# Layer 2's modulation summed partly by VectorE in the dense experts; first projection and S5's weights woven

## The chip, the cores and the metric

One core of one Trainium2 chip. The metric is the device time of one execution in microseconds, as a median of runs. The engines are TensorE (PE, matrix products), VectorE (DVE), ScalarE (ACT), GpSimd (POOL) and SyncE (SP, which here issues the weight loads). They run in parallel, each in its own program order, and wait for each other only through semaphores.

## The reference

Two blocks, each of two layers, on one sequence of 256 tokens with 1024 columns, all fp32. The change touches the first block, whose layer is:

```python
c_act = jax.nn.silu(c)
for layer in range(DEPTH):
    mod = c_act @ mod_w[layer] + mod_b[layer]
    sh_m, sc_m, gt_m, sh_f, sc_f, gt_f = jnp.split(mod[:, None, :], N_MOD, axis=-1)
    h = x * (1 + sc_m) + sh_m
    u, q, k, v, g_out, a_low = jnp.split(h @ w_in[layer], IN_SPLITS, axis=-1)
    y_s5 = _s5_group(u, ...)
    y_gla = _gla_group(q, k, v, g_out, a_low, ...)
    y = jnp.concatenate([y_s5, y_gla], axis=-1) @ w_out[layer]
    x = _layer_norm(DN_ALPHA * x + (1 + gt_m) * y, ...)
    h = x * (1 + sc_f) + sh_f
    ...
    f = _swiglu(h, ...) if layer % 2 == 0 else _moe_swiglu(h, ...)
    x = _layer_norm(DN_ALPHA * x + (1 + gt_f) * f, ...)
```

`c` is one row of 1024 values and `mod_w` is 2 x 1024 x 6144, so each layer's modulation is a product of one row with 24 MB of weights. S5 is a state space model with 32 groups (its weights are built from small parameters by elementwise work and transposes), GLA a gated linear attention with 4 heads. Layer 1 has a dense feed-forward part of width 3584 ("dense experts" below), layer 2 eight sparse experts of which two are chosen per token. The second block has two layers with three kinds of attention, a memory attention and a feed-forward part of width 4096.

## The kernel before, in words

**Products in fp32.** Each weight tile of 128 x 1024 values is split: ACT copies it to a high part (`his`, L303, tile WH), DVE subtracts that from the original to get a low part (`los`, L312, tile WL), and PE makes three products (`mm3`, L207: high by high, high by low, low by high). Weights come through a ring of five slots of 1 MB (tile RG), planned as one list of loads in the order of use (`plan`, L246); `fetch` (L291) lets SP issue a load once the load five places before it in the list has been released by DVE (or, for raw loads that PE reads as they are, by PE). Four pairs of conversion buffers lie between the ring and PE: ACT writes one when PE has released it.

**Modulation.** The 6144 columns of a layer are twelve blocks of 512. For each block PE multiplies the eight 128-row parts of two raw loads by one column of silu(c) (`pe_mod`, L517) into one PSUM bank; ACT copies the row out and sends it to DRAM (`a_mod`, L531). Shifts and scales come back as columns (`a_cols`, `pe_cols`, `v_cols`, L543 to L559), the two gates as rows spread over the partitions, to which DVE adds bias and 1 (`a_gate` L567, `v_gate` L575). Blocks 0 to 3 of layer 1 come in the start; blocks 4 to 11 of layer 1 and 0 to 3 of layer 2 in the first mixer stage; blocks 4 to 11 of layer 2 in the second.

**Stages.** A fence (L159) makes every engine wait for every other. Before the first mixer stage: a start (S5's parameter rows, `v_s5_rows`, L990; input weights, `v_s5_in`, L1129; four blocks of modulation), a fence, the first projection (`pe_project`, L620, with S5's fourteen transposing and multiplying jobs of layer 1 between its column blocks, `pe_s5_jobs`, L1082), and then S5's output weights on DVE (`v_s5_out`, L1159). S5's weights of layer 2 are built by DVE in the first mixer stage (input) and in the first three blocks of the dense experts (output).

**Mixer stages.** S5, GLA, the modulation and, in the first, S5's next input weights are strands: generators whose pieces end at a `yield`. `weave` (L324) gives each engine its own order of pieces, written out as a string (`ORDERS`, L335): s is S5 (`pe_s5` L1184, `v_s5` L1235, `a_s5` L1280), g GLA (`pe_gla` L708, `v_gla` L790, `a_gla` L893), m modulation (`pe_mods` L1315), b S5's next weights. A piece that has to wait blocks what stands behind it on its engine. GLA makes two halves of four score groups: fourteen small products of PE, which DVE masks (freeing the banks), sums, and hands back to PE for the output. The attention stages of the second block are woven in the same way.

**Dense experts.** `pe_ffn` (L1529), `v_ffn` (L1550) and `a_ffn` (L1572): seven blocks, each gate, up and the last block's down product, twelve conversions of 1024 columns.

## Time and profile before

| what | value |
| --- | --- |
| median of 3 runs | 3159.86 us (3159.57 to 3163.46) |
| profiled execution: its own time | 3157.04 us |
| its span | 3155.2 us, mean granted TensorE clock 0.887 |
| PE busy | 2614.9 us (83%) |
| DVE busy | 2082.6 us (66%) |
| ACT busy | 1563.1 us (50%) |
| POOL busy | 41.3 us (1%) |
| moved by DMA | 601.73 MB, 191 GB/s over the span |

Busy time is the time in which an engine has an instruction in work; issuing DMAs and waiting are not counted. In a timeline a line is a run of like instructions: its start in us from the span's start, its length, the engine, the line of the program (of a helper, mostly: L167 is a tensor by tensor operation of DVE, L197 an activation, L205 a product, L213 a transpose), written tile and read tiles, shapes, the count, and in brackets how long the engine was idle before it and what ended that. The clock is a share of 2.4 GHz; its lower level is 0.5.

### The profile page before, as it was taken

What the parts mean: (1) busy time and instruction counts of PE and PEld (TensorE: products, weight loads), DVE (VectorE), ACT (ScalarE), POOL (GpSimd) and SP (SyncE); (2) the same over time, 40 slices, a digit from 0 to 9 for tenths busy, and PEclk for the clock granted to TensorE, in tenths of its full rate; (3) what the DMA queues carried; (4) which work ended last, traced back from release to release, by engine and by line L of the source; (5) the groups of instructions that cost most, each with busy time, mean ns of one, the idle gap of its engine ahead of it and who ended that gap; (6) DMA issues with size and microseconds to landing.
All of it is one profiled execution on the core that took longest, in us unless ns stands there. A gap on an engine that the chain in (4) does not pass through costs nothing.

```text
span 3155.2 us, 31903 instructions
## 1 busy us (share of the span) xinstructions
PE 2614.9 (83%) x11806; PEld 2005.0 (64%) x11806; DVE 2082.6 (66%) x2374; ACT 1563.1 (50%) x1909; POOL 41.3 (1%) x45
## 2 busy tenths in 40 slices
PE   4879669969965999999999999948676998676898
PEld 1724558858354777777777777736355786445687
DVE  5476566554655788887878888865764554675454
ACT  1221434433133777787877778743434444333443
POOL 0001000000100000000000000000000000000000
PEclk9879879988976999999999999978577998767799
DMA  7345325542521898998989989954012554203252
GB/s 228 105 140 173 129 73 191 192 141 82 196 98 67 307 350 316 338 330 305 357 303 343 333 328 346 343 187 137 0 54 80 174 185 140 75 14 107 80 184 96
DMA packets 281490, 601.73 MB, mean 191 GB/s; under 512 B 29456, under 2 KB 36440, under 8 KB 281200
## 3 DMA queue, kind: packets, MB, share of 16 engines
q1 hardware_dynamic: 257264, 580.30, 52.3%
q10 hardware_dynamic: 24064, 19.34, 2.2%
q8 instruction: 94, 1.54, 0.2%
q14 instruction: 68, 0.56, 0.1%
HBM read 598.48 MB, written 1.11 MB: 190 GB/s over the span
## 4 chain that ended last, share of the span: by engine, by line
PE 63%; DVE 22%; ACT 9%; issue 2%; ACTq 2%; DMA 1%; POOL 0%; DVEq 0%; POOLq 0%; PEldq 0%
PE PS L205 61%; DVE WL L167 6%; ACT WH L197 3%; PE PS L213 2%; DVE WF L167 2%; DVE AR L167 2%; ACT AR L197 2%; ACTq L146 1%; DVE HF L167 1%; DVE MW L167 1%; ACT MW L197 1%; DVE SMALL L178 1%; DVE HTR L167 1%; DVE MOD L167 1%; DVE AR L175 1%
## 5 line engine op out<-in xcount | busy, mean ns | idle before, releaser
L167 DVE TENSOR_TENSOR WL<-RG,WH 128x1024 fp32r<-128x1024 f32 (+1 forms) x558 | 919.4, 1648 | 528.0 <-ACT WH L197 508.4
L197 ACT ACTIVATE WH<-RG 128x1024 fp32r<-128x1024 f32 x782 | 827.3, 1058 | 610.0 <-PE PS L205 549.4
L205 PE MATMUL PS<-WH,HTR 128*128 128x512 f32 (+3 forms) x2920 | 927.6, 394 | 74.8 <-DVE HTR L167 33.0
L205 PEld LDWEIGHTS PS<-WH,HTR 128*128 128x128 f32 x2920 | 558.6, 194 | 209.3 <-DVE HTR L167 35.5
L205 PE MATMUL PS<-WL,HTR 128*128 128x512 f32 (+3 forms) x1460 | 569.0, 390 | 0.0
L205 PE MATMUL PS<-WH,ATR 128*128 128x512 f32 x1624 | 522.5, 395 | 7.3 <-DVE ATR L167 7.3
L205 PEld LDWEIGHTS PS<-WH,ATR 128*128 128x128 f32 x1624 | 309.5, 191 | 74.9 <-DVE WL L167 8.4
L205 PE MATMUL PS<-MW,HTR 128*128 128x512 f32 x1332 | 329.9, 397 | 18.1 <-DVE MW L167 18.1
L205 PE MATMUL PS<-WL,ATR 128*128 128x512 f32 x812 | 320.0, 394 | 0.0
L205 PEld LDWEIGHTS PS<-WL,HTR 128*128 128x128 f32 x1460 | 283.5, 194 | 52.9
L167 DVE TENSOR_TENSOR MW<-RG,MW 128x2048 fp32r<-128x2048 f32 x112 | 256.7, 2292 | 64.2 <-ACT MW L197 54.0
L205 PEld LDWEIGHTS PS<-MW,HTR 128*128 128x128 f32 x1332 | 248.1, 190 | 70.6 <-DVE MW L167 20.2
L197 ACT ACTIVATE MW<-RG 128x1024 fp32r<-128x1024 f32 x224 | 237.9, 1062 | 24.8 <-PE PS L205 1.8
L213 PE MATMUL PS<-KC,AR 128*128 128x128 f32 (+1 forms) x704 | 127.5, 319 | 117.5 <-DVE AR L167 51.2
L205 PE MATMUL PS<-RG,SMALL 128*1 128x512 f32 x384 | 180.5, 621 | 33.2 <-DVE SMALL L167 28.4
L213 PEld LDWEIGHTS PS<-KC,AR 128*128 128x128 f32 (+1 forms) x704 | 99.5, 165 | 145.8 <-DVE AR L167 58.7
L205 PEld LDWEIGHTS PS<-WL,ATR 128*128 128x128 f32 x812 | 154.9, 191 | 31.4
L205 PEld LDWEIGHTS PS<-RG,SMALL 128*1 128x1 f32 x384 | 30.4, 86 | 159.9 <-issue 120.9
L213 PE MATMUL PS<-KC,X 128*128 128x128 f32 x160 | 35.3, 410 | 111.4 <-POOL X L167 36.3
L197 ACT ACTIVATE AR<-PS 128x512 f32<-128x512 f32 (+3 forms) x122 | 67.9, 556 | 97.3 <-PE PS L205 52.1
L213 PEld LDWEIGHTS PS<-KC,X 128*128 128x128 f32 x160 | 31.6, 221 | 115.6 <-DVEq L155 60.8
L197 ACT ACTIVATE ATR<-PS 128x512 fp32r<-128x512 f32 x102 | 61.1, 599 | 80.4 <-PE PS L213 75.5
(207 smaller groups left out, 2106.1 us busy)
## 6 DMA issues: line engine op xcount, KB each, us to landing
RG<-in_moe_w_gate SPq DMA_DIRECT2D x112, 1024.0 KB, 5.2
RG<-in_moe_w_up SPq DMA_DIRECT2D x112, 1024.0 KB, 5.6
RG<-in_moe_w_down SPq DMA_DIRECT2D x112, 1024.0 KB, 5.7
RG<-in_w_ff SPq DMA_DIRECT2D x64, 1024.0 KB, 5.2
RG<-in_mod_w SPq DMA_DIRECT2D x48, 1024.0 KB, 5.1
RG<-in_w_in SPq DMA_DIRECT2D x36, 1024.0 KB, 5.2
RG<-in_w_out SPq DMA_DIRECT2D x16, 1024.0 KB, 5.0
RG<-in_ffn_w_gate SPq DMA_DIRECT2D x14, 1024.0 KB, 5.0
```

The source lines that it names most:

```text
L146: return Ins(self.e.dma_start(dst, src, **kw) if self.e is not None else None, self)
L167: return self.did(lambda: self.e.tensor_tensor(o, a, b, op))
L175: return self.did(lambda: self.e.scalar_tensor_tensor(out=o, in0=a, scalar=s, in1=b, op0=op0, op1=op1))
L178: return self.did(lambda: self.e.tensor_reduce(out=o, in_=a, op=op, axis=AX.X))
L197: return self.did(lambda: self.e.activation(o, a, f, bias=bias, scale=scale))
L205: return self.did(lambda: self.e.matmul(o, l, r, start=start, stop=stop))
L213: return self.did(lambda: self.e.transpose(o, a, perm))
```

## The change

It does the following.
- **Start.** The fences around the first projection go. Modulation, columns and projection of layer 1 are one strand (p), S5's rows, input weights and jobs another (r), woven as a stage of its own ("start"). ACT's first exponential stands before most of its load issues.
- **S5's output weights** of layer 1 become part of strand b in the first mixer stage.
- **Modulation of layer 2.** Of its twelve blocks, eight (columns 0 to 2047 and the two gates) are no longer multiplied by PE. Sixteen loads of 1 MB with 128 rows each are planned among the dense experts' loads, and DVE adds each, times its values of silu(c), into accumulators cleared at the stage's start. The partial sums over the partitions are finished by PE: the columns by sixteen products with a column of ones in block 4 of the dense experts, the gates by four products with a matrix of ones in the second mixer stage. Blocks 6 to 9 stay as they were, in the second mixer stage. The first mixer stage keeps blocks 4 to 11 of layer 1 alone.
- **Orders.** All strings are written anew, the attention stages' too.

```diff
-    ("mixers0", "a"): "mgsbggmgssgmbmmmmgmgggggmsmmgggggggmmmgsmmgsgmsss",
+    ("mixers0", "a"): "gmsbmsbgmgsggmmmmmggggggmsmmsggggsgggsmssggg",
...
-    ("mixers0", "pe"): "ggmmsmmsmmgmmsmmgmmggmggmsssmmggssssggsmsggmgmggmmsggmggmggmggmgssssssssmsssms",
-    ("mixers0", "v"): "gsmbggggsgsgssssggbbggbggbgggbgggggggmsggggggggggggggggggggsgmmggssmss",
...
+    ("mixers0", "pe"): "mmggsmmsmmmmsmmgsmmgmggmggmsmssggssssggsssggsssggsssgsmssssggggggggg",
+    ("mixers0", "v"): "bggsbgsgbgsmgssssgbbggbggbggbgggggggggsggggggsgggggmgmsggmggsggssgggggg",
...
-    ("mixers1", "pe"): "sggsmmgmmsmgmggmggmsssmggmggmggsmggmgmssssmggssssggsssggsmggssgssssmm",
-    ("mixers1", "v"): "gsmbsgggsgggssssggggggggggggggggggggggggggsgggggggsgggsgmmsgsgms",
...
+    ("mixers1", "pe"): "sggsmmgsssgsgsggsgssssssssssssmsggmsggmsggsggmgsmmggmggmggmggmgmm",
+    ("mixers1", "v"): "sgmbsgggsgggssssggmgggggggggggmgssgmsgmgggggggsggsggsggggggggggggm",
...
+    ("start", "a"): "rprrrpppprrrppppprrrrrpppppppppppppppppppppp",
+    ("start", "pe"): "ppprpppprpprrrrrppprpprrrrppprpppprprrpppppppppp",
+    ("start", "v"): "rpprrrrrrrrrrrrppppprrppppprpprppprppppprprrpppppppppp",
...
+        SUMS = ((0, 2048),), ((2048, 1024), (5120, 1024))
+        def plan_sums(i):
+            for k in (i % 4 * 2, i % 4 * 2 + 1):
+                row = w["mod_w"][1, k * 128:(k + 1) * 128, :].rearrange("p (a n) -> p a n", a=2)
+                src = (row[:, 0:1, 0:2048], row[:, :, 2048:3072])[i // 4]
+                m = len(SUMS[i // 4])
+                W.plan(("sums", i, k), src, m, 2048 // m, raw=W.raw_added)
+        SUMS_BY = (), (0,), (1, 2), (3,), (4, 5), (6,), (7,)
...
-            plan_mod(l, 4, 12)
             if l == 0:
-                plan_mod(1, 0, 4)
+                plan_mod(0, 4, 12)
+            else:
+                plan_mod(1, 6, 10)
...
+                        for i in SUMS_BY[n]:
+                            plan_sums(i)
...
+        def v_sums_clear(v):
+            for at in (HROW, GTM, ROWT):
+                x = v.ms(at, 0.0)
+            x.then_inc(sums_v, "clear")
+        def a_sums_in(a):
+            a.wait_ge(sums_v, 0, "clear")
+            for group, dsts in zip(SUMS, SUMS_AT):
+                for (c, n), at in zip(group, dsts):
+                    a.dma(at[0:1, :], w["mod_b"][1:2, c:c + n]).then_inc(sums_in)
+        def v_sums(v, i):
+            g = i // 4
+            v.wait_ge(sums_in, 3)
+            for k in (i % 4 * 2, i % 4 * 2 + 1):
+                ld = W.of["sums", i, k][0]
+                v.wait_ge(W.landed[ld.slot], ld.use)
+                for m, at in enumerate(SUMS_AT[g]):
+                    x = v.stt(at, ld.dst[:, m, :], sm(24 + k, 1), at, MUL, ADD)
+                x.then_inc(W.raw_added)
+        def pe_sums(pe, ready):
+            pe.wait_ge(*W.of["sums", 3, 7][0].raw)
+            ready()
+            for j in range(16):
+                x = pe.mm(PS[:, 5, j:j + 1], HROW[:, j * 128:(j + 1) * 128], COL[:, 1:2], True, True)
+            x.then_inc(sums_pe)
+        def a_sums(a):
+            a.wait_ge(sums_pe, 1)
+            a.act(MC[:, 48:56], PS[:, 5, 0:8], ACT.Copy)
+            a.act(MC[:, 56:64], PS[:, 5, 8:16], ACT.Identity, bias=1.0).then_inc(sums_a)
+        ROW_SUMS = [(GTM, GTM, h) for h in range(2)] + [(ROWT, GTF, h) for h in range(2)]
+        def pe_row_sums(pe):
+            for i, (src, dst, h) in enumerate(ROW_SUMS):
+                yield
+                if i:
+                    pe.wait_ge(sums_v, 0, f"row{i - 1}")
+                pe.mm(PS[:, 3, :], KC[:, K_ONE:K_ONE + 128], src[:, h * 512:(h + 1) * 512], True, True).then_inc(
+                    sums_pe, f"row{i}")
+        def v_row_sums(v):
+            for i, (src, dst, h) in enumerate(ROW_SUMS):
+                yield
+                v.wait_ge(sums_pe, 0, f"row{i}")
+                v.ts(dst[:, h * 512:(h + 1) * 512], PS[:, 3, :], 1.0, None, ADD).then_inc(sums_v, f"row{i}")
...
+                if l == 0 and i == 1:
+                    pe.wait_ge(sw_v, 0, "PC")
...
+        def pe_mods(pe, l):
+            if l:
+                yield from pe_row_sums(pe)
+                yield
+                pe.wait_ge(sums_v, 0, "row3")
+            for n in (range(6, 10) if l else range(4, 12)):
+                yield from pe_mod(pe, l, n)
+            pe_cols(pe, 1 + l)
+        def v_mods(v, l):
+            if l:
+                yield from v_row_sums(v)
+            yield
+            v_cols(v, 1 + l)
             if l == 0:
-                yield [(1, n) for n in range(4)], 2
-        def pe_mods(pe, l):
-            for some, k in chunks(l):
-                for x in some:
-                    yield from pe_mod(pe, *x)
-                pe_cols(pe, k)
-                yield
-        def v_mods(v, l):
-            for some, k in chunks(l):
-                yield
-                v_cols(v, k)
-            yield
-            v_gate(v, l, 2, GTM)
-            yield
-            v_gate(v, l, 5, GTF)
+                yield
+                v_gate(v, 2, GTM)
+                yield
+                v_gate(v, 5, GTF)
...
+        def v_s5_next(v):
+            yield from v_s5_out(v, 0)
+            yield from v_s5_in(v, 1)
...
+                beside = n == sums
+                pe_up(pe, W.of[gate(n)], 4, ready,
+                      (lambda: pe_sums(pe, lambda: pe.wait_ge(ffn_v, r - 1, "lo0"))) if beside else None)
+                if beside:
+                    pe.wait_ge(sums_a, 1)
...
-                W.los(v, 4 if up is None else 8)
+                W.los(v, 4)
+                beside(n)
+                if up is not None:
+                    W.los(v, 4)
...
+        def pe_first(pe):
+            yield
+            pe.wait_ge(first_in, 3)
+            pe.tr(PS[:, 7, 0:96], CB[0:96, 128:256], KC[0:96, K_ID:K_ID + 96]).then_inc(pro_pe)
+            for n in range(4):
+                yield from pe_mod(pe, 0, n)
+            pe_cols(pe, 0)
+            yield
+            pe.wait_ge(pro_v, 1)
+            yield from pe_w_in(pe, 0)
+        def pe_w_in(pe, l):
+            yield from pe_h_mod(pe, 2 * l)
+            yield from pe_project(pe, ("w_in", l), INC1, FIRST[l], lambda k: pe.wait_ge(hm_v, 2 * l, f"l{k // 2}"))
+        def v_first(v):
+            yield
+            v.wait_ge(pro_pe, 1)
+            v.cp(MB, PS[:, 7, 0:96]).then_inc(pro_v)
+            yield
+            v_cols(v, 0)
+            for _ in range(4):
+                yield
+                W.los(v, 1)
+            yield from v_w_in(v, 0)
+        def v_w_in(v, l):
+            yield from v_h_mod(v, 2 * l, l, 1)
+            yield from v_project(v, ("w_in", l), INC1, PR1, AHEAD1)
+        def a_first(a):
+            for n in range(4):
+                yield
+                a_mod(a, 0, n)
+            yield
+            a_cols(a, 0)
+            for _ in range(4):
+                yield
+                W.his(a, 1)
+            yield from a_w_in(a, 0)
+        def a_w_in(a, l):
+            for dst, src in ((ROWS[:, O_HG:O_HG + 512], rowb(w["gla_head_gain"][l, :])),
+                             (ROWS[:, O_LMG:O_LMG + 1024], rowb(w["ln_mix_g"][l, :])),
+                             (ROWS[:, O_LMB:O_LMB + 1024], rowb(w["ln_mix_b"][l, :])),
+                             (SMALL[:, 40:42], w["gla_b_alpha"][l, :].rearrange("(c p) -> p c", p=128)),
+                             (ST[0:16, 128:384], w["gla_w_alpha_up"][l, :, :])):
+                a.dma(dst, src).then_inc(rows_in)
+            yield from a_h_mod(a, 2 * l)
+            yield from a_project(a, ("w_in", l), INC1, PR1, AHEAD1)
+        def pe_s5_first(pe):
+            yield from pe_s5_rows(pe)
+            yield from pe_s5_jobs(pe, 0, S5_BANKS[0], JOBS)
+        def v_s5_first(v):
+            yield from v_s5_rows(v)
+            yield from v_s5_in(v, 0)
+            yield
+            v_s5_cx(v, 0)
+            yield from v_s5_jobs(v, 0, S5_BANKS[0], JOBS)
+        def a_s5_first(a):
+            yield from a_s5_rows(a)
+            yield from a_s5_jobs(a, 0, S5_BANKS[0], JOBS)
...
+                    v_sums_clear(v)
                     s5w = v_s5_out(v, 1)
-                    v_ffn(v, *ffn1()[1:], 7, 0, lambda: run(s5w, 1))
+                    v_ffn(v, *ffn1()[1:], 7, 0, lambda: run(s5w, 1), lambda n: v_beside(v, n))
```

## Rows read from the trace of the kernel before

**Rows 1.** Busy time of each engine by stretch; its first line names the columns

```profile
core 0: us, PE busy (x) PEld busy (x) DVE busy (x) ACT busy (x) POOL busy (x), PEclk, DMA share, GB/s
...
152.00:178.80 26.80, 0.00 (x0) 0.00 (x0) 25.38 (x38) 0.00 (x0) 0.00 (x0) 0.59 0.00 0
178.80:341.20 162.40, 145.72 (x768) 64.84 (x768) 108.44 (x169) 35.77 (x54) 8.87 (x12) 0.93 0.55 172
432.90:682.70 249.80, 241.01 (x1064) 198.52 (x1064) 145.48 (x145) 107.19 (x113) 0.00 (x0) 0.98 0.51 173
762.30:905.00 142.70, 123.29 (x704) 65.80 (x704) 91.79 (x135) 33.42 (x50) 8.87 (x12) 0.86 0.40 133
1012.00:2140.00 1128.00, 1031.74 (x4630) 833.50 (x4629) 919.94 (x566) 848.89 (x913) 5.82 (x4) 0.97 0.87 315
2158.00:2326.00 168.00, 119.46 (x448) 81.80 (x447) 113.66 (x253) 61.16 (x119) 0.00 (x0) 0.69 0.15 48
```

**Rows 2.** Timeline of the start, ScalarE and TensorE: start us, length us, what

```profile
5.18 13.11 ACTq L146 DMA_DIRECT2D MOD<-in_s_b_im  x1
...
27.77 0.20 ACT L197 ACTIVATE HF<-HF 32x2 f32<-32x2 f32 x1
...
30.42 0.65 ACT L197 ACTIVATE HF<-HF 32x128 f32<-32x128 f32 x2
...
28.37 9.78 PE L205 MATMUL PS<-RG,SMALL 128*1 128x512 f32 x16 [28.37 <-DVE SMALL L167]
```

**Rows 3.** Timeline of the start, TensorE and VectorE, to the first projection

```profile
38.83 7.03 PE L205 MATMUL PS<-RG,SMALL 128*1 128x512 f32 x16 [0.68 <-ACT MOD L197]
...
69.35 0.17 DVE L167 TENSOR_TENSOR SMALL<-PS,SMALL 128x16 f32<-128x16 f32 x1 [2.30 <-PE PS L213]
...
73.88 5.21 DVE L167 TENSOR_TENSOR WL<-RG,WH 128x1024 fp32r<-128x1024 f32 x4 [4.16 <-ACT WH L197]
...
84.44 0.79 PE L205 MATMUL PS<-WH,HTR 128*128 128x512 f32 x1 [10.93 <-DVE HTR L167]
```

**Rows 4.** Timeline of TensorE in the first projection, three of S5's jobs

```profile
97.39 1.47 PE L213 MATMUL PS<-KC,AR 128*128 128x128 f32 x12
```

**Rows 5.** Timeline of VectorE in the first mixer stage

```profile
208.80 2.48 DVE L167 TENSOR_TENSOR HF<-AR,PS 128x1024 f32<-128x1024 f32 x2 [4.82 <-PE PS L205]
...
228.62 0.69 DVE L181 COPY WF<-PS 128x512 f32<-128x512 f32 x1
...
251.03 10.14 DVE L167 TENSOR_TENSOR WF<-WF 128x128 f32<-128x128 f32 x18
263.40 1.28 DVE L167 TENSOR_TENSOR MOD<-PS,KC 128x512 f32<-128x512 f32 x2 [2.23 <-PE PS L205]
```

**Rows 6.** Timeline of TensorE in both mixer stages, one score group each

```profile
293.97 1.82 PE L205 MATMUL PS<-WF 64*128 64x128 f32 x14 [2.44 <-DVE WF L167]
...
825.29 2.82 PE L205 MATMUL PS<-WF 64*128 64x128 f32 x14 [2.03 <-DVE WF L167]
```

**Rows 7.** Timelines of VectorE and ScalarE in the dense experts, and one clearing

```profile
480.44 1.23 DVE L167 TENSOR_TENSOR WL<-RG,WH 128x1024 fp32r<-128x1024 f32 x1 [1.49 <-ACT WH L197]
...
482.06 1.06 ACT L197 ACTIVATE WH<-RG 128x1024 fp32r<-128x1024 f32 x1 [1.66 <-PE PS L205]
...
185.16 0.91 DVE L187 MEMSET WF<- 128x1024 f32 x1 [0.28 <-DVE WF L181]
```

**Rows 8.** The page: a group of VectorE's (busy, mean ns), the modulation's loads

```profile
L167 DVE TENSOR_TENSOR MW<-RG,MW 128x2048 fp32r<-128x2048 f32 x112 | 256.7, 2292 | 64.2 <-ACT MW L197 54.0
...
RG<-in_mod_w SPq DMA_DIRECT2D x48, 1024.0 KB, 5.1
```

**Rows 9.** Timelines of ScalarE and VectorE at the end of the second mixer stage

```profile
878.68 0.59 ACT L197 ACTIVATE MOD<-PS 1x512 f32<-1x512 f32 x1 [10.14 <-PE PS L205]
...
894.44 0.17 DVE L167 TENSOR_TENSOR SMALL<-PS,SMALL 128x16 f32<-128x16 f32 x1
...
902.12 1.22 DVE L167 TENSOR_TENSOR MOD<-MOD,ROWS 128x1024 f32<-128x1024 f32 x1 [1.59 <-DMA ROWS<-in_mod_b]
```

More of the change, by code:

```diff
@@ L321, in los, with run @@
         self.next_lo += n
+def run(strand, pieces=None):
+    if pieces is None:
+        for _ in strand:
+            pass
+    else:
+        for _ in range(pieces):
+            next(strand, None)
 def weave(eng, stage, **strands):
@@ L644, in a_project @@
                 parts = W.of[(*key, j)]
-                W.his(a, ahead[j])
+                for _ in range(ahead[j]):
+                    yield
+                    W.his(a, 1)
+                yield
                 a.wait_ge(W.used, parts[-1].i + 1)
@@ L1504, in build, with pe_up @@
         ffn_pe, ffn_v, ffn_a = signal("ffn_pe"), signal("ffn_v"), signal("ffn_a")
-        def pe_up(pe, parts, b0, ready):
-            for p in parts:
+        def pe_up(pe, parts, b0, ready, mid=None):
+            for j, p in enumerate(parts):
+                if j == 2 and mid is not None:
+                    mid()
                 pe.wait_ge(W.lo, p.los)
@@ L1527, in pe_down, with pe_ffn @@
                 x.then_inc(W.used)
-        def pe_ffn(pe, gate, up, down, nblk, r0, ready):
+        def pe_ffn(pe, gate, up, down, nblk, r0, ready, sums=None):
             for n in range(nblk):
@@ L1570, in v_ffn, with a_ffn @@
             W.los(v, 4)
[L1572 removed]
+        def a_ffn(a, gate, up, down, nblk, r0, scale=lambda t: 1.0, ready=lambda: None, beside=nothing):
             for n in range(nblk):
@@ L2705, in build, with v_beside, a_beside @@
         S5_BANKS = (0, 1, 2), (4, 5, 6, 7)
-        def run(strand, pieces=100):
-            for _ in range(pieces):
-                next(strand, None)
+        def v_beside(v, n):
+            for i in SUMS_BY[n]:
+                v_sums(v, i)
+        def a_beside(a, n):
+            if n == 0:
+                a_sums_in(a)
+            if n == 4:
+                a_sums(a)
         def ffn1():
@@ L2912, in g_program @@
             for l in range(L):
-                g.fence(ends)
+                if l:
+                    g.fence(ends)
                 g.fence(ends)
```

230 lines of the change are left out of this document (114 added, 116 removed).

## The prediction

> **What bounds the kernel now.** I read the stages first: busy time of each engine in stretches cut where all engines meet [rows 1]. TensorE (PE) is busy in nearly all of most stages, but not everywhere: from 152.0 to 178.8 us it does nothing while VectorE (DVE) works 25.4 us. The two mixer stages take 162.4 and 142.7 us, PE busy for 145.7 and 123.3 of them, DVE for 108.4 and 91.8. The dense experts (249.8 us) are PE's: 241.0 us busy, DVE only 145.5. So the change takes PE work from stages where PE is fullest and puts DVE work where DVE has 104 us free. Then I read each engine's timeline there, to see who waits for whom.
>
> **Part 1, the start.** ScalarE (ACT) issues loads first: one of the small-packet loads of S5 holds its queue 13.11 us, and it reaches the exponential of dt at 27.8 us [rows 2]. Only c's exponential moves ahead of that; a weave puts the row copy of the first modulation block behind ACT's S5 steps. I take the issues to end where they do now (same bytes), dt's exponential near 28, ACT's tanh and sines (till 31.1 now, 3.3 us [rows 2]) by 32, and the first row copy at 32.3, which lets PE begin its second block at 33 instead of 38.8 [rows 3]. PE's own first block moves from 28.4 [rows 2] to about 21, when x has landed. The other three blocks cost 7.03 us of PE and 1.3 us of handover each [rows 3]: the fourth ends near 56, 6 us sooner. But S5's twelve transposes now stand behind the third block, near 48, a little later than today, so DVE ends building S5's inputs near 67 and does the column sums (69.35 now [rows 3]) at 67.5. Then, without fence or ACT's five issues: four lows, 5.2 us [rows 3]; S5's C scaling 1.4; half of h, 5.0: PE's projection starts at 79.1, not 84.4 [rows 3]. It lasts 67.6 us now, to 152.0 [rows 1, 3]. Ten of S5's fourteen jobs leave it for PE's wait (three take 1.47 us [rows 4]: 4.9 us), and some 2 us of waiting for the K jobs go: 60.7, end 139.8. S5's output weights leave too (26.8 us [rows 1]). Mixers begin at 140 instead of 178.8: **-38**. Bounds: -42 (ACT's issues end earlier, without which nothing moves) and -28 (PE's in-order pieces wait for ACT's copies of the B jobs).
>
> **Part 2, the first mixer stage.** PE loses four blocks, 28 us: 145.7 becomes 118. DVE gains 25.4: 108.4 becomes 134, and it becomes the bound. Walking DVE's string: pieces b1, b2, b3 (8.7, 8.7, 6.8 us, the work of the stretch before [rows 1]) stand between the gate's first steps, so phases come from ACT at about 34, and S5's scan block starts at 37.5 after the stage's start (now 208.8 - 178.8 = 30.0) and takes 19.8 us [rows 5], to 57.3. From there DVE runs nearly dense as now, 228.6 to 261.2, 32.6 us, with the ten microseconds of levels at its end [rows 5]: 90. Four score groups follow. Each is 1.82 us of PE [rows 6], then DVE's mask, 1.28 us [rows 5], which alone frees the banks, with small S5 products between instead of a half block of modulation, 3.5 us, half of [rows 3]'s 7.03: 3.5 us a group, not 6. With the last output 16 us: 106. Levels of the second half 10.5: 117. The second four are slowed by both gates, columns and S5's finish placed between (8 us of DVE): 22, so 139. The norm and its product take 11.5 more: 150.5. I add half a microsecond of fences: 151, against 162.4: **-11**. Bounds: 143 (DVE's 134 and the 9 us it must wait in the tail) and 168 (if each in-order string adds as much idle time as DVE has now, 54 us less what PE's leaving gives back, about 20): -19 to +6.
>
> **Part 3, the dense experts.** Sixteen 1 MB loads join 42. Data: 173 GB/s now; with them some 240, where the sparse experts move 315 [rows 1]. Ring: each load is still issued when the fifth before it is released. DVE: sixteen loads of 128x2048 multiply-adds at 2.3 us [rows 8] (two of 1024: 2.5), 38 us, of the 104 free. What matters is the burst. PE frees one of four conversion buffers each 2.72 us [rows 7]; ACT's high part and DVE's low part are ready 2.4 us later, PE needs them after 3 x 2.72 = 8.2. So DVE has 5.8 us of slack, and its own regular pause of 1.5 before it: an insertion of 7.3 us is free. Blocks 1, 3, 5, 6 insert 4.6 to 5.0: nothing, hidden by those buffers; without them they would cost 19 us. Block 2 inserts 9.2 us right after having made up the lateness of S5's piece: 3.1 us late. Block 4 inserts 10: 2.8. The clearing (4096 columns at 0.91 us per 1024 [rows 7], 3.6 us) stands before the first low parts, that have 2 us to spare: 1.6. PE's sixteen one-column products with 128x128 weights, 32 passes at the 0.12 us of a 128-column pass [rows 4]: 3.5, counted whole, since PE is the bound here. Sum **+11**; bounds +4 and +22 (half of those 19 us exposed as well).
>
> **Part 4, the second mixer stage.** Four blocks of PE (28 us) give way to four 512-column products (0.9 each) and four DVE adds of 0.7. Before the levels the state chain loses its half blocks of modulation: -5.5. The first four scores hold one half block instead of five: -9 more. The second four hold four, as tight as today or 3 us worse. So the second half's output is ready 11 to 14 us earlier than 886. The two gate sums with their loads (last at 902.1, after waiting for a landing [rows 9]) are gone. The columns remain: 15.8 us from the last row copy (878.7) to the sum at 894.4 [rows 9], but with idle engines about 9: both chains end near 890, and the stage lasts 130 us instead of 142.7: **-13**, bounds -19 and -4 (the row's two DMA legs keep their 15.8 us).
>
> **Part 5, reordered attention.** Same instructions in another order, 168 us, PE 119, DVE 114, clock 0.69 [rows 1]: waits set it, on no one engine. No row prices an order: I take 0 and keep -4 to +4 for each of the two.
>
> GpSimd's work and queue are untouched; SP's queue only gets the sums' loads in ring order.
>
> **Sum.** -38 - 11 + 11 - 13 = -51 us, against the profiled execution's 3157.0: 3106. The runs' median is 2.8 us above that execution; the prediction is for a median: 3109.
>
> **The clock.** The score groups show both levels: fourteen products take 1.82 us at the full granted clock and 2.82 in the second mixer stage at 825.3, after PE had stood 2 us idle [rows 6]; the first mixer stage holds 0.93 in the mean, the second 0.86 [rows 1]. The change makes PE less busy exactly here. The Trainium skill (TensorE: Matmul & The Clock Gate, What's actually happening) says the half rate is the default and activity is what lifts it. By that rule the modulation's products also served to keep the clock up, and the sum would be 15 us worse, as in the second rival. From the rows alone: PE with 118 us of work in 151 would be nearly as dense as in today's second stage (123 in 143, mean 0.86), where groups run at both levels; I keep 1.82 in the sum and give the other level a rival of its own.
>
> **Rivals.**
> - *DVE's strings bind.* The moved 25 us come back whole in the first mixer stage, since each piece stands in order ahead of something that ACT or PE waits for: that stage 166 instead of 151. 3124. For it: DVE would be 89% busy in my 151, and it is at 67% now. Against: its idle time now is mostly spent waiting for PE. 17%.
> - *The clock falls*: eight score groups per stage at 2.82 plus transposes and state products, 9 us in the first mixer stage and 6 in the second: 3124 as well. 12%.
> - *Tighter than walked*: start -42, first mixers -18, second -19, experts +4: 3085. 8%.
> - *Slower.* The place is the ring in the dense experts. If DVE reaches each sums load before it has landed, it stands in order for a landing of 5.1 us [rows 8] plus 2.4: 120 us, less 44 hidden by six blocks' slack, 76 instead of 11: 3174. It decides from (62 + 44)/16 = 6.6 us a load. Against it: a load is issued four releases ahead, and releases are 5.4 us apart. 4%.
> - *The moved work does not shorten the stages*: the mixers' ends hang on row copies and landings, not on PE, and only S5's place counts, eaten by the experts' delays: 3152 to 3163. 3%.
>
> **How the numbers follow.** The forecast has 56% (3095 to 3123). The range leaves out the slower rivals and the last of the tight one, and takes the terms' bounds, which will not all fall on one side: 3084 to 3136. A difference of 0.2% (6 us) is about what a measurement of this kernel tells from none. Faster 0.94, within 0.02, slower 0.04.
>
> **What would show it.** Right: the first PE transposes of the mixers near 140; DVE above 85% busy in a stage of some 150 us; score groups 3.5 us apart; the dense experts about 261 us with PE pauses of 3 us in blocks 2 and 4 and a few in block 4's gate; the second mixer stage near 130 us and ending with the column sums. Wrong: PE waiting in the experts for DVE in every block, or DVE's waits there on landings; 2.8 us score groups; a first mixer stage over 162 us; an attention stage moved by more than 4 us.

## The result, and the profile after the change

The changed kernel takes 3120.48 us in the median of four runs (3114.61 to 3121.96); the kernel before took 3159.72 beside it (four runs, 3153.53 to 3163.46). The ratio is 0.9874 with a 95% interval of 0.9854 to 0.9895: faster by some 39 us, where the prediction had 51 and a range of 3084 to 3136. The profiled execution took 3114.61 us, 42.4 less than the profiled one of before; stage by stage it goes like this (a stage begins with the first work after a fence):

| stretch | before | after | difference | predicted |
| --- | --- | --- | --- | --- |
| start, to the first mixer stage | 178.8 | 133.8 | -45.0 | -38 |
| first mixer stage | 162.5 | 156.4 | -6.1 | -11 |
| GLU, output, norm | 91.7 | 91.8 | +0.1 | 0 |
| dense experts, to the transposes after their norm | 269.9 | 288.1 | +18.2 | +11 |
| second projection | 59.6 | 60.0 | +0.4 | 0 |
| second mixer stage | 142.6 | 132.6 | -10.1 | -13 |
| all the rest, both attention stages in it | 2252.1 | 2252.0 | -0.1 | 0 |

Busy time by stretch, with the columns of [rows 1], for the start, the first mixer stage, the dense experts without their norm, the second mixer stage and a stretch of 168 us in the first attention stage:

```profile
0.00:133.80 133.80, 101.34 (x439) 65.86 (x440) 71.04 (x145) 33.39 (x45) 0.30 (x5) 0.92 0.62 197
133.80:290.20 156.40, 125.48 (x704) 67.14 (x704) 130.97 (x199) 32.17 (x50) 8.86 (x12) 0.84 0.40 125
382.00:649.90 267.90, 249.38 (x1096) 204.01 (x1096) 188.37 (x171) 107.54 (x115) 0.00 (x0) 0.97 0.63 224
730.10:862.60 132.50, 98.57 (x647) 62.16 (x647) 89.47 (x135) 29.79 (x45) 9.14 (x12) 0.78 0.20 64
2115.00:2283.00 168.00, 115.99 (x450) 79.93 (x449) 114.83 (x253) 60.81 (x119) 0.00 (x0) 0.71 0.14 45
```

Against [rows 1] the reader is to see two things. In the first mixer stage DVE is now 84% busy, as walked; but PE lost only 20 us of busy time, though four blocks of 7.03 us left it, and its mean clock fell from 0.93 to 0.84. In the second the clock fell from 0.86 to 0.78. In the dense experts PE is busy 8.4 us longer, for 4.0 us of added products.

**The start.** The timelines of ACT, PE and DVE, the lines that answer to [rows 2, 3]:

```profile
10.22 10.11 ACTq L146 DMA_DIRECT2D MOD<-in_s_b_im  x1
...
26.07 0.20 ACT L197 ACTIVATE AR<-AR 32x2 f32<-32x2 f32 x1 [18.72 <-issue]
...
28.30 0.65 ACT L197 ACTIVATE AR<-AR 32x128 f32<-32x128 f32 x2
...
29.68 7.03 PE L205 MATMUL PS<-RG,SMALL 128*1 128x512 f32 x16 [1.16 <-ACT MOD L197]
...
63.15 0.17 DVE L167 TENSOR_TENSOR SMALL<-PS,SMALL 128x16 f32<-128x16 f32 x1
...
75.64 0.79 PE L205 MATMUL PS<-WH,HTR 128*128 128x512 f32 x1 [2.40 <-DVE HTR L167]
```

The issues end at 26.0, where they ended before, but the table load and c's exponential no longer stand behind them, and ACT is through with the sines at 28.95. So PE's second block begins at 29.7 where I had 33. DVE begins to build S5's inputs right behind dt's exponential, at 26.3, and stands still only 1.0 us before the column sums (63.15, for 67.5), so the projection begins at 75.6 where I had 79.1. It lasts 57.8 us; I had 60.7.

**The first mixer stage.** PE in the first half (state chain and scores), then the second half's score groups, the answer to [rows 6], and DVE between them; then the clock of that last stretch:

```profile
172.04 7.03 PE L205 MATMUL PS<-RG,SMALL 128*1 128x512 f32 x16 [2.82 <-ACT MOD L197]
...
187.20 9.04 PE L205 MATMUL PS<-RG,SMALL 128*1 128x512 f32 x16
...
197.34 7.03 PE L205 MATMUL PS<-RG,SMALL 128*1 128x512 f32 x16
...
225.99 3.32 PE L205 MATMUL PS<-WF 64*128 64x128 f32 x14 [2.76 <-DVE WF L167]
...
232.58 1.83 PE L205 MATMUL PS<-WF 64*128 64x128 f32 x14
...
256.99 3.35 PE L205 MATMUL PS<-WF 64*128 64x128 f32 x14 [2.56 <-DVE WF L167]
261.71 3.35 PE L205 MATMUL PS<-WF 64*128 64x128 f32 x14 [1.38 <-DVE MOD L167]
...
267.67 3.35 PE L205 MATMUL PS<-WF 64*128 64x128 f32 x14 [1.16 <-DVE MOD L167]
```

```profile
264.27 1.23 DVE L167 TENSOR_TENSOR MOD<-MOD,ROWS 128x1024 f32<-128x1024 f32 x1 [0.90 <-DMA ROWS<-in_mod_b]
```

```profile
257.00:282.00 25.00, 20.03 (x76) 17.06 (x76) 19.72 (x23) 2.39 (x4) 0.00 (x0) 0.50 0.13 43
```

After three idle stretches of PE (7.6 us before 186.6, then 2.76, then 2.56) its work runs at half pace at first: the same sixteen products take 9.04 us and then 7.03. It isn't so after every one: the block at 172.0, behind 2.82 us of idle time, takes its 7.03. After 257 PE stays at the lower clock to the stage's end, 25 us at a granted clock of 0.50: a score group takes 3.35 us where it took 1.82 in the same place before.

**The dense experts.** PE's pauses in order of time, with the one-column products and what follows them; then DVE and ACT in block 2:

```profile
396.81 0.50 PE L205 MATMUL PS<-WH,HTR 128*128 128x512 f32 x1 [1.84 <-DVE WL L167]
...
473.61 0.50 PE L205 MATMUL PS<-WH,ATR 128*128 128x512 f32 x1 [3.90 <-DVE WL L167]
...
526.13 4.02 PE L205 MATMUL PS<-SMALL,H 128*128 128x1 f32 x32
...
530.58 0.63 PE L205 MATMUL PS<-WL,HTR 128*128 128x512 f32 x1
...
536.56 0.39 PE L205 MATMUL PS<-WL,HTR 128*128 128x512 f32 x1
...
540.17 0.50 PE L205 MATMUL PS<-WH,HTR 128*128 128x512 f32 x1 [1.62 <-ACT SMALL L197]
...
553.13 0.50 PE L205 MATMUL PS<-WH,ATR 128*128 128x512 f32 x1 [1.78 <-DVE WL L167]
```

```profile
462.50 9.73 DVE L175 SCALAR_TENSOR_TENSOR H<-RG,SMALL,H 128x2048 f32<-128x2048 f32 x4
...
467.62 2.22 ACT L197 ACTIVATE WH<-RG 128x1024 fp32r<-128x1024 f32 x2 [7.10 <-DMA RG<-in_ffn_w_down]
```

The pauses of blocks 2 and 4 are there (3.9 and 1.8 us, for 3.1 and 2.8), and so is the clearing's (1.84, for 1.6). Blocks 1, 3, 5 and 6 show none. What I had not priced stands behind the one-column products: 5.7 us of products at 0.63 us each where 0.39 is usual, and 1.6 us of waiting for ACT's copies of their sums.

### The profile page after: what moved, and what is told of

The parts are those of the page before. It is cut to its first block, busy times and chain, and to the rows that moved or that the text cites. A ratio compares the mean times of both kernels' runs of the same rounds, so it can differ in the third digit from the quotient of the medians.

```text
span 3112.8 us, 31727 instructions
## 1 busy us (share of the span) xinstructions
PE 2572.9 (83%) x11717; PEld 2004.8 (64%) x11717; DVE 2122.7 (68%) x2399; ACT 1553.6 (50%) x1899; POOL 41.5 (1%) x45
## 4 chain that ended last, share of the span: by engine, by line
PE 61%; DVE 24%; ACT 9%; issue 2%; ACTq 1%; DMA 1%; POOL 0%; DVEq 0%; POOLq 0%; PEldq 0%
PE PS L205 59%; DVE WL L167 6%; ACT WH L197 3%; DVE AR L167 2%; PE PS L213 2%; ACT AR L197 2%; DVE MOD L167 2%; DVE WF L167 1%; DVE MW L167 1%; ACTq L146 1%; ACT MW L197 1%; DVE SMALL L178 1%; DVE HF L167 1%; DVE HTR L167 1%; DVE AR L175 1%
## 5 line engine op out<-in xcount | busy, mean ns | idle before, releaser
L205 PEld LDWEIGHTS PS<-MW,HTR 128*128 128x128 f32 x1332 | 248.2, 190 | 70.7 <-DVE MW L167 20.3
L197 ACT ACTIVATE MW<-RG 128x1024 fp32r<-128x1024 f32 x224 | 237.9, 1062 | 24.6 <-PE PS L205 1.6
L213 PE MATMUL PS<-KC,AR 128*128 128x128 f32 (+2 forms) x716 | 129.6, 319 | 98.5 <-DVE AR L167 49.4
L213 PEld LDWEIGHTS PS<-KC,AR 128*128 128x128 f32 (+2 forms) x716 | 99.8, 164 | 129.7 <-DVE AR L167 50.6
L205 PEld LDWEIGHTS PS<-WL,ATR 128*128 128x128 f32 x812 | 154.9, 191 | 31.8
L205 PE MATMUL PS<-RG,SMALL 128*1 128x512 f32 x256 | 119.3, 617 | 8.7 <-ACT MOD L197 4.7
L205 PE MATMUL PS<-AR 128*128 128x128 f32 (+2 forms) x240 | 59.8, 390 | 40.6 <-ACT AR L198 18.8
```

Of the source, the lines that this page charges most:

```text
L197: return self.did(lambda: self.e.activation(o, a, f, bias=bias, scale=scale))
L205: return self.did(lambda: self.e.matmul(o, l, r, start=start, stop=stop))
L213: return self.did(lambda: self.e.transpose(o, a, perm))
```

## Experiments

All start from the changed kernel. Totals are medians of four runs (five for the last), the ratio is to the kernel before on the same chip; since the same start came out between 132.6 and 136.1 us long from one execution to the next, parts are judged by the length of their stage and not by totals. Each run has one profiled execution, and stages that were left as they are differ too: the dense experts took 288.0 to 288.1 us in the changed kernel and in e6 and e8 to e11, but 284.5 and 284.6 in e5 and e7; the second mixer stage took 132.4 to 135.6. "Experts" runs from their first product to the transposes after the norm (288.1 in the changed kernel), "first mixers" to ACT's first copy behind the stage (156.4).

| run | total | ratio (95%) | stage |
| --- | --- | --- | --- |
| changed kernel | 3120.5 | 0.9874 (0.9854 to 0.9895) | |
| e1_spread | 3112.6 | 0.9854 (0.9832 to 0.9876) | experts 281.5 |
| e2_products | 3115.6 | 0.9859 (0.9835 to 0.9883) | experts 281.2 |
| e3_no_sums | 3100.0 | 0.9809 (0.9790 to 0.9828) | experts 268.7 |
| e4_pool | 3119.6 | 0.9876 (0.9856 to 0.9895) | experts 284.4 |
| e5_gate_late | 3118.3 | 0.9859 (0.9832 to 0.9886) | first mixers 155.3, experts 284.5 |
| e6_filler | 3113.7 | 0.9845 (0.9817 to 0.9874) | first mixers 156.9 |
| e7_filler_gate | 3115.0 | 0.9842 (0.9814 to 0.9869) | first mixers 154.9, experts 284.6 |
| e8_s5out_back | 3134.8 | 0.9907 (0.9881 to 0.9933) | start 161.7, first mixers 154.0 |
| e9_small_filler | 3125.1 | 0.9883 (0.9861 to 0.9905) | first mixers 157.6 |
| e10_copy_early | 3119.6 | 0.9857 (0.9834 to 0.9880) | second mixers 134.3 |
| e11_jobs_last | 3129.1 | 0.9889 (0.9867 to 0.9911) | start 146.8 |
| e12_best | 3104.3 | 0.9825 (0.9809 to 0.9841) | experts 271.4 |

### What the sums cost in the dense experts

**e3_no_sums** leaves the sums out, and with them layer 2's shift, scale and gates.

```diff
-        SUMS_BY = (), (0,), (1, 2), (3,), (4, 5), (6,), (7,)
+        SUMS_BY = ((),) * 7
-                    pe_ffn(pe, *ffn1(), 7, 0, lambda k: None, 4)
+                    pe_ffn(pe, *ffn1(), 7, 0, lambda k: None)
-                    v_sums_clear(v)
```

> The dense experts without any of the sums: no clearing, no sums loads, no adds, no one-column products; layer 2's shift, scale and gates are then not those of the reference (the columns are set to zero, the rows keep what their tiles hold). Everything else stays as in the changed kernel. Theory: all of the stage's growth (267.9 against 249.8) is theirs: stage 250, total 3102.5. Rival: a part of it comes from what the new order of loads and stages did besides (S5's output weights on VectorE meeting a fuller memory): stage 254 or more, total 3106 or more.

Measured: 268.7, 19.4 us less than with the sums and 1.2 less than before the change; the first product and the first transpose behind the norm are

```profile
385.08 0.80 PE L205 MATMUL PS<-WH,HTR 128*128 128x512 f32 x1 [5.60 <-DVEq L155]
...
653.80 1.51 PE L213 MATMUL PS<-KC,X 128*128 128x128 f32 x6 [22.60 <-POOLq L155]
```

The growth of the stage is all theirs. The 1.2 us are no gain: behind the last pause of PE in the stage, products run at the lower clock in the kernel before and in the changed one, and the way from there to the transposes takes them 35.4 us for 33.7 in this run.

**e1_spread** spreads the same sixteen loads (numbered singly).

```diff
-        SUMS_BY = (), (0,), (1, 2), (3,), (4, 5), (6,), (7,)
+        SUMS_BY = ((0, 1), (2, 3), (4, 5), (6, 7), (8, 9, 10), (11, 12, 13), (14, 15))
```

> The sixteen sums loads are spread 2, 2, 2, 2, 3, 3, 2 over the seven blocks instead of 0, 2, 4, 2, 4, 2, 2; same loads, same adds, same products. The changed kernel has two pauses of PE of 3.9 us (blocks 2 and 4), a dense-expert stage of 267.9 us and 3120.5 us in the median. Theory of the bursts (only an insertion of more than 7.3 us on VectorE is seen by PE): both pauses go, a small one of under 1 us may come with the three-load insertions (7.1 us), stage 260 to 262, total 3113. Rival, volume (each sums load costs by its 1 MB and its 2.35 us wherever it stands): stage 266 to 268, total 3120.

Measured: 281.5, 6.5 us less. The two pauses are gone, and of the three-load insertions (7.1 us of DVE and more) one left a pause:

```profile
580.36 0.50 PE L205 MATMUL PS<-WH,ATR 128*128 128x512 f32 x1 [0.99 <-DVE WL L167]
```

So it is the burst that costs, not the load: the same 16 MB and 39 us of adds, in portions of about what four conversion buffers cover, are nearly free. The volume theory falls. Of the 6.5 us the pauses are 4.7 (3.90 and 1.78 gone, 0.99 come); an earlier wait, for S5's transposes, grew from 3.2 to 4.3. The rest lies where PE's products ran at the lower clock for less long, and that differs by as much in stages left as they are.

**e2_products** moves the one-column products behind the last down product.

```diff
-                    pe_ffn(pe, *ffn1(), 7, 0, lambda k: None, 4)
+                    pe_ffn(pe, *ffn1(), 7, 0, lambda k: None)
+                    pe_sums(pe, nothing)
...
+            H_ = HL if r == 1 else H
-                    v.tt(H[:, t, c], PS[:, 2 * t + h, :] if acc is None else acc[:, t, c], gt[:, c], MUL)
+                    v.tt(H_[:, t, c], PS[:, 2 * t + h, :] if acc is None else acc[:, t, c], gt[:, c], MUL)
```

> The sixteen one-column products leave block 4's gate and stand behind the last down product, in the post-LN where PE waits 26 us anyway; the post-LN's scratch moves to another tile for it. Theory: in block 4 the products cost PE 4.0 us themselves, 2.5 us more because the gate's next products run at the lower clock (0.63 us instead of 0.39 each for 5.7 us), and 1.6 us of waiting for ScalarE; all 8 us go: stage 260, post-LN and second projection as long as before (80.2), total 3112.5. Rival, only the products' own time counts (the slow products after them were a pause that comes anyway): 4 us, total 3116.5. Second rival: what leaves block 4 comes back in the post-LN, whose stretch grows by 4 us: total 3116.5 with a stage of 260.

Measured: 281.2, 6.9 us less, and the norm's stretch is not longer: PE makes them in 3.63 us and then still waits 19.14.

```profile
642.00 3.63 PE L205 MATMUL PS<-SMALL,H 128*128 128x1 f32 x32
664.76 1.51 PE L213 MATMUL PS<-KC,X 128*128 128x128 f32 x6 [19.14 <-POOLq L155]
```

Of the 8.1 us expected, 1.9 came back: the burst of block 4 now shows in full, as a pause of 3.70 instead of 1.78, since the products had given DVE time to catch up. Products, clock and ACT's copy are worth 7 to 9 us here, not the 3.5 that I had reckoned.

The clock's part of it doesn't come each time. e5 and e7 have these products in their old place, and there the clock stayed up; in e5:

```profile
526.08 3.63 PE L205 MATMUL PS<-SMALL,H 128*128 128x1 f32 x32
529.56 0.49 PE L205 MATMUL PS<-WH,HTR 128*128 128x512 f32 x1
529.89 0.40 PE L205 MATMUL PS<-WL,HTR 128*128 128x512 f32 x1
...
536.93 0.50 PE L205 MATMUL PS<-WH,HTR 128*128 128x512 f32 x1 [1.63 <-ACT SMALL L197]
```

From the products' start to the end of the wait for ACT it is 10.9 us in both, and 14.0 in the changed kernel (526.13 to 540.17). These 3.2 us are the clock's; 5.3 are the products and the wait.

**e4_pool** clears on GpSimd.

```diff
-                    v_sums_clear(v)
...
+                if l == 0:
+                    v_sums_clear(g)
```

> The three clearings (1.76, 0.91 and 0.91 us on VectorE) go to GpSimd, which is idle in this stage. Theory: the pause of 1.84 us that PE has before block 0's up half goes, and nothing else: stage 266, total 3118.6. Rival: VectorE makes up its lateness anyway before the burst of block 2, so the whole gain is given back there or the clearing on GpSimd slows VectorE's own operations: stage 267.9, total 3120.5.

Measured: 284.4, 3.7 us less, but no less than in e5 and e7, where nothing in this stage was changed. What the rows tie to the clearing is the pause of 1.84 us, which is gone, and 2.2 us up to S5's transposes. The rest is the clock's: behind the transposes 1.8 us are lost again up to the one-column products, 1.6 are won behind them, and 1.7 behind the last pause, where the products of the changed kernel ran at the lower clock. The total's gain is inside its interval.

### What holds the first mixer stage

**e5_gate_late**: in DVE's string the fourth m moves from before the 37th g to before the 43rd.

```diff
-    ("mixers0", "v"): "bggsbgsgbgsmgssssgbbggbggbggbgggggggggsggggggsgggggmgmsggmggsggssgggggg",
+    ("mixers0", "v"): "bggsbgsgbgsmgssssgbbggbggbggbgggggggggsggggggsgggggmgmsggggsggssggmgggg",
```

> First mixer stage: in VectorE's order the second gate's sum moves from between the second half's score groups to after the fourth, where VectorE waits 2.67 us for the stage's last output; everything else stays. In the changed kernel VectorE stands at this sum for a bias row that lands at 264.27, with the score groups behind it. Theory of the gate: the wait of 0.9 us and the 1.94 us of the sum leave the chain, stage 156.4 to 153.5, total 3117.5. Rival, the clock alone: the groups are paced by their 3.35 us on PE and the chain closes up elsewhere, gain under 1 us: 3120.

Measured: 155.3, 1.1 us less (the unchanged strings gave 155.9 to 157.5). The wait for the bias row is gone, but the groups stay 4.7 us apart, paced by 3.35 us of PE and 1.3 of DVE's mask. Nearly the rival. And the next stretch gives it back: from the stage's start to the first product of the dense experts it is 248.1 us (132.6 to 380.7), in the changed kernel 248.2.

**e6_filler** and **e7_filler_gate** keep PE working beside the second half's scores with products that nobody reads.

```diff
+                    if l == 0 and c and i:
+                        fill(2)
...
+                if l == 0 and c:
+                    fill(6)
                 pe.wait_ge(gla_v, l, "st21")
```

> First mixer stage, second half of the scores: PE gets twelve products of one column by 512 whose result nobody reads, six (2.6 us at the full clock) where it stood idle before the first group and two (0.9 us) before each of the other three. Theory of the clock: the granted clock of 0.50 that holds from 257 to 282 us in the changed kernel followed PE's idle 2.56 us; with the filler it stays near 1.0, the groups take 1.82 us instead of 3.35, and of the 4 x 1.5 us some 4 come off the end although PE does more (the gate's landing at 264 still stands): stage 152.5, total 3116.5. Rival, strings of VectorE: the groups wait for VectorE's masks, sums and gates anyway, the clock is a symptom: stage 156 to 158, total 3120 to 3122.

> Both edits, the filler products and the second gate's sum moved behind the scores. If clock and gate each hold the same groups one after the other: 156.4 - 3 - 5 = 148.5 for the stage and 3112.5 in total. If one hides the other: as the better of the two alone.

Measured: 156.9, the rival's figure, and 154.9, hardly less than e5's 155.3. In the second of them the groups and the clock are

```profile
260.21 1.82 PE L205 MATMUL PS<-WF 64*128 64x128 f32 x14
261.96 1.88 PE L205 MATMUL PS<-KC,SMALL 128*1 128x512 f32 x4
263.77 1.83 PE L205 MATMUL PS<-WF 64*128 64x128 f32 x14
...
272.56 1.82 PE L205 MATMUL PS<-WF 64*128 64x128 f32 x14
```

```profile
257.00:282.00 25.00, 20.39 (x96) 11.21 (x94) 21.22 (x26) 3.14 (x4) 0.01 (x1) 0.91 0.13 43
```

The filler does hold the clock (0.91 for 0.50, groups of 1.82 for 3.35), and from the first group to DVE's work on the last output it is 20.2 us (260.2 to 280.4) against 23.2 without it (255.9 to 279.1 in e5_gate_late), three times 1.88 us of filler included. But its own six products hold the first group back by 2.6 us, and up to the experts' first product it is 248.1 us again. The totals of both runs are lower than the changed kernel's by more than that (6.8 and 5.5 us by the medians, 9 and 10 by the ratios); the mixer stage doesn't account for it, and e7's experts, 3.5 us shorter without an edit, do so only in part. One filler product is 0.88 us, not 0.44 as I had written: the trace shows two records for each.

**e9_small_filler** is e7 with `fill(2)` and `fill(1)`.

> As the run with filler and late gate, but two filler products before the first score group and one before each of the others. A filler product took 0.88 us, not the 0.44 I had reckoned, so six of them held the first group back by 3 us (260.2 instead of 257.0) and two each added 1.9 us between groups. Theory (the clock does hold the groups, the filler ate what it gave): the groups keep 1.82 us, the first stands at 257 as in the changed kernel, the spacing falls from 4.4 to VectorE's 3.6 to 4.0, and the stage takes 151 to 152.5, total 3114. Rival (VectorE paces them at any clock): stage 154 to 156, total 3118.

Measured: 157.6. With two products the first group is quick, then PE waits 1.93 us for a mask, the clock falls (0.65 in the mean of that stretch), and the last two groups take 3.35 us again. So in this stage the clock and PE's work are one account: what keeps the clock up costs about what the clock gives. In the kernel before, half blocks of modulation stood between these groups, which took 1.82 us; they had to be made anyway.

**e8_s5out_back** puts S5's output weights back behind the projection.

```diff
-            yield from v_s5_out(v, 0)
             yield from v_s5_in(v, 1)
...
             weave(v, "start", p=v_first(v), r=v_s5_first(v))
+            run(v_s5_out(v, 0))
```

> S5's output weights (25.4 us of VectorE) back in the start, behind the projection, where they stood in the kernel before; nothing else changes but that VectorE's string in the first mixer stage lacks these three pieces. Theory (the move is worth having because VectorE has room beside PE in the mixers): the start grows by 25.4 to 159.2, the first mixer stage's scan block starts 7 us earlier, as before, and the stage takes 149.5: net +18.5, total 3139. Rival (VectorE's strings bind): what leaves the mixers comes off their end whole, stage 131, total 3120.5. Between them: each us by which the stage falls short of 149.5 is one that VectorE's string bound.

Measured: start 161.7 (PE idle 24.6 us before it), first mixers 154.0, as busy as this:

```profile
161.70:315.70 154.00, 128.07 (x704) 67.97 (x704) 107.87 (x167) 32.15 (x50) 8.87 (x12) 0.82 0.40 127
```

DVE has 23 us less to do there, and the stage is only 2.4 us shorter: its scan block comes 33.7 us after the stage's start instead of 36.7, and the rest goes as before. So the pieces moved there do not bind this stage, and these 25 us are hidden under the mixers all but 2.4: the rival of DVE's strings falls, and so does my own 7 for the late scan block. That holds for the pieces ahead of the scan block, which are what this run takes out; from the scan block's end to the end of the levels DVE stands idle for only 2.4 of 35.7 us in the changed kernel and 2.7 of 36.0 here, so there its string does bind. The totals show less, 14 us by the medians and 10 by the ratios: the profiled execution of this run was the highest of its four (3143.6), that of the changed kernel the lowest of its own (3114.6), and the start alone varies by 3.5 us. The stage lengths are the firmer reading for the mixers, since the first mixer stage of kernels with the same strings differed by 1.6 us at most; what the move is worth in the total, 10 to 25 us, stays open between the two.

### The start and the second mixer stage

**e11_jobs_last** moves S5's fourteen jobs behind the projection in all three strings.

```diff
-    ("start", "pe"): "ppprpppprpprrrrrppprpprrrrppprpppprprrpppppppppp",
+    ("start", "pe"): "ppprpppprppppppppppppppppppppppppprrrrrrrrrrrrrr",
```

> Start: S5's fourteen jobs all behind the projection instead of before and between its products; the rest of the weave stays. Theory (the weave hides the jobs): the projection begins 3 us earlier and is 7.6 us shorter without the jobs between, but the fourteen jobs then stand alone, about 1.2 us each with their copies: mixers begin at 138 to 142 instead of 133.8, total 3126. Rival (PE's own time is what counts, wherever the jobs stand): 133 to 135, total 3120.

Measured: mixers begin at 146.8, 13 us later. The projection begins at 75.7 as in the changed kernel, so the jobs ahead of it were hidden there; it ends at 128.6, 4.8 us sooner (133.4 there); and the jobs alone take 18 us, more than expected.

**e10_copy_early** moves ACT's copy of the second stage's first modulation block ahead of an exponential and a tanh.

```diff
-    ("mixers1", "a"): "sgmbssggggsggsggggsgggssggsmggmmggmmg",
+    ("mixers1", "a"): "sgmbssggggsggsggggsgggssgmgsggmmggmmg",
```

> Second mixer stage: ScalarE's copy of the first modulation block moves ahead of one exponential and one tanh, so that PE can begin the next block when the bank is free, at 817.4, and not at 821.0. Theory (PE is dense from there to the last row copy, so each us of its wait is one of the stage): PE's idle 3.67 us becomes under 1, the stage shortens by 3, from 132.5 to 129.5, total 3117.5. Rival (the score groups wait for the levels of VectorE, ready at 824.2, and the modulation is only moved from one gap to another): no gain, 132 to 133.

Measured: 134.3, no gain (132.4 to 135.6 in the other runs). The block moves forward, and PE waits at the next place, for DVE's levels, with the first group 94.6 us after the stage's start as in the changed kernel (94.5):

```profile
820.16 3.59 PE L205 MATMUL PS<-RG,SMALL 128*1 128x512 f32 x8 [0.68 <-ACT ROWS L197]
...
826.78 1.97 PE L205 MATMUL PS<-WF 64*128 64x128 f32 x14 [3.03 <-DVE WF L167]
828.67 5.10 PE L205 MATMUL PS<-RG,SMALL 128*1 128x512 f32 x8
```

Behind this wait the next half block takes 5.10 us for 3.59, at the lower clock, which makes up most of the 1.8 us by which the stage is longer than the changed kernel's.

### A better version

**e12_best** is e1, e2, e4 and e5 together.

> The four edits that shortened their stage, together: sums spread 2, 2, 2, 2, 3, 3, 2; one-column products behind the last down product; clearings on GpSimd; second gate's sum behind the scores. If they add: dense experts 288.1 (from their first product to the next stage's first) less 6.5, 6.9 and 2.2, so 272.5 where the kernel without any sums has 268.7; first mixer stage 1 us shorter; total 3120.5 - 16.5 = 3104. Rival (spread and products share one lateness: what the products delayed gave VectorE time to catch up): 276 to 279 and 3108 to 3111.

Measured: 3104.3, ratio 0.9825 (0.9809 to 0.9841), 16 us under the changed kernel and 56 under the one before. The experts take 271.4, 2.7 us more than without any sums; two pauses of 0.99 us are left in them.

```profile
381.79 0.79 PE L205 MATMUL PS<-WH,HTR 128*128 128x512 f32 x1 [5.79 <-DVEq L155]
...
536.54 0.50 PE L205 MATMUL PS<-WH,ATR 128*128 128x512 f32 x1 [0.99 <-DVE WL L167]
571.37 0.50 PE L205 MATMUL PS<-WH,ATR 128*128 128x512 f32 x1 [0.99 <-DVE WL L167]
...
653.16 2.15 PE L213 MATMUL PS<-KC,X 128*128 128x128 f32 x9 [19.13 <-POOLq L155]
```

## Why the prediction was right, and where it was not

The sign, the range and the mechanism held: work of PE and DVE left the stages where it stood alone or in the way, and came to stand beside other work. The sum was 8.6 us too good against the profiled execution (-51 for -42.4), and 11.5 against the medians. That it came so near was partly luck: the start gave 7 us more than the sum had, and everything behind it 15.6 us less (+2.6 where it had -13). By its steps:

- **Start, -38: in fact -45, below its bound of -42.** The issues ended where I had them, but I let dt's exponential follow at 28 and the sines end at 32, as if ACT's table load still stood behind the issues. It had moved ahead with c's exponential (26.07 and 28.95): 3.3 us, which DVE's string of S5's inputs, begun that much sooner and with 1.0 us of waiting in it, carries to the column sums and the projection's start. The projection itself was 3 us shorter than the sum had it. e11 shows that weaving the jobs is worth 13 us; I had priced the ten jobs between products at 4.9 and the waits for K at 2. (The walk's own figures, 178.8 to 139.8, give -39 and not -38.)
- **First mixer stage, -11: in fact -6.** The walk was right to 57 us (the scan block 36.7 us after the start for 37.5, through with it at 56.5 for 57.3). The failed step is the one after: "from there DVE runs nearly dense as now, 32.6 us" became 35.7, and the first four score groups took 20.8 for 16. In both the rows show PE at its lower clock after a wait: 2.0 us on the first modulation block, 1.5 on the first group and about as much on the S5 products next to it. For the first of these e2, whose strings here are the same, is the test, since its clock was up at that block:

```profile
190.55 7.03 PE L205 MATMUL PS<-RG,SMALL 128*1 128x512 f32 x16
```

There the 35.7 us are 33.8, and DVE's waits in them 0.5 us for 2.4. For the groups it is read from the rows alone. The second half took 23.8 for 22, its 3.35 us groups made up for in part by the shorter tail.
- **The clock.** This is the rival I had at 12%, with 9 us in this stage; the rows above show 2.0 on the block, 3.0 around the first group and, by e7 against e5, 3.0 in the second half. It did not replace the forecast, because the second mixer stage's groups ran at the full clock (1.80 where one of before took 2.82 [rows 6]), but in the first stage it came, and the final time of 3120.5 is nearer to that rival's 3124 than to 3109. By the rule of the Trainium skill (TensorE: Matmul & The Clock Gate, What's actually happening), under which activity lifts the clock, the trace agrees: taking products away and leaving pauses in their place gave back part of what it saved. e6, e7 and e9 show that these fillers do not buy it back.
- **Dense experts, +11: in fact +18.** Bursts and clearing came nearly as reckoned: insertions up to 7 us free, the two of 9 to 11 us seen (3.9 and 1.8 us, or 3.7 without the products ahead of the second; I had 3.1 and 2.8), clearing 1.8 for 1.6. The failed term is the sixteen one-column products "at 3.5, counted whole" (32 passes at its own 0.12 are 3.8): they took 4.0, were followed by 5.7 us at the lower clock (a product followed the last after 0.43 us instead of 0.23: 2.6 us), and made PE wait 1.6 for ACT. e2 takes 6.9 us out. Pauses, products and clock together are 15.8 of the 18.2; the rest I can't put to single rows, but e3 shows that it is the sums' too. In e5 and e7 the same stage cost 3.5 us less, by the clock alone: a sum for it has that much play.
- **Second mixer stage, -13: in fact -10.** The columns' path and the missing gate sums came as walked. The second four score groups, "as tight as today or 3 us worse", were 6.8 us worse (28.5 us from the first PE work to the output for 21.7): half a block of modulation stands before each group. e10 rules out ACT's late copy as the cause. That the half blocks themselves are it was only read, not tried.
- **Attention, 0:** from the first transposes to the next fence it took 151.8 and 151.7 us, where the same stages took 152.4 and 151.5 before.
- **The slower rival** (each sums load waits for its landing) didn't come: DVE showed no wait on a landing of the sums. A landing did hold ACT for 7.10 us in block 2, on the down weights, which SP could only issue once the up halves were released; it ended with the burst and cost nothing of its own there. **DVE's strings**: the moved pieces bind nothing by e8; behind the scan block DVE was dense, as the walk had it, but for 2.4 us.

## What to carry to other kernels

Work handed to an engine with free time cost here mainly by its largest portions and not by its sum: reckon the slack that the buffers give at that place, and cut the work into portions below it (here 7 us; e1 alone took 6.5 off a cost of 19 us, and with the products and the clearing moved too, 3 were left). Small products of few columns belong where PE waits anyway, since they cost their own time, that of who reads them, and in most of these executions the pace of the products behind them. And before taking products out of a stage with pauses, look whether its pace hangs on the granted clock: what leaves there may give back less than its length.

## What the runs showed of the hardware that I had not expected

- PE's granted clock fell without any pause of PE, at the end of sixteen fp32 products of one column with 128x128 weights, back to back for 4.0 us; the products after them ran at 0.50 until 536, then at full clock again. It was so in the changed kernel and in e6 and e8 to e11 (for half as long in e1 and e4), but not in e5 and e7, where the same products ran at 1.00 and so did the ones behind them:

```profile
526.10:530.00 3.90, 3.90 (x33) 3.87 (x32) 1.23 (x1) 1.06 (x1) 0.00 (x0) 0.90 0.24 97
530.00:532.00 2.00, 2.00 (x6) 1.61 (x7) 0.00 (x0) 0.00 (x0) 0.00 (x0) 0.50 0.94 254
```

The same stretch in e5:

```profile
526.00:529.70 3.70, 3.70 (x35) 3.66 (x34) 1.22 (x1) 1.06 (x1) 0.00 (x0) 1.00 0.23 93
529.60:536.00 6.40, 5.71 (x25) 4.37 (x25) 1.23 (x1) 1.72 (x2) 0.00 (x0) 1.00 0.52 165
```

- PE can stay at the lower clock for 25 us while it is busy for 20 of them (the stretch 257 to 282 above).
- GpSimd clears 128x2048 fp32 in 1.80 us, as quick as DVE's 1.76.
- The same start took 132.6 to 136.1 us from one execution to another, the same dense experts 284.5 to 288.1: a gain of a few us needs the row that it comes from, beside the length of its stage.
